# Second attention: the sum of squares of each head as one row, with a column of ones as weights

## What is computed

```python
    for blk in range(s // Q_BLOCK):
        ...
        weights = probs[:, :, 0] - lam * probs[:, :, 1]
        outs.append(jnp.einsum('bhqk,bkhe->bqhe', weights.astype(v.dtype), vb))
    o = jnp.concatenate(outs, axis=1)
    o = rms_norm(o, head_norm_g) * (1.0 - lam_0)      # mean of o*o over the 128 values of a head
    o = o.reshape(b, s, BRANCH) * jax.nn.silu(z)
    return x + o @ w_out
```

## Time and profile before

| what | value |
|---|---|
| median of 3 runs | 1300.03 us (1299.74 to 1300.12) |
| the profiled execution, its own time | 1300.48 us |
| its span in the trace | 1298.7 us |
| PE busy | 1289.9 us (99%), 7158 matmul records |
| PE weight loads busy | 1087.7 us (84%) |
| DVE busy | 793.3 us (61%) |
| ACT busy | 612.4 us (47%) |
| POOL busy | 299.9 us (23%) |
| DMA | 130.35 MB, mean 100 GB/s |

### The profile page before, as it was taken

The page is one execution under the profiler, slowest core; times in us unless marked ns, Lnnn a source line. Parts: engine busy times, 40 slices in busy tenths (PEclk is TensorE's granted clock), DMA queues, the critical chain, the costliest instruction groups (busy, mean ns, idle before and its releaser), DMA issues.

```text
span 1298.7 us, 18343 instructions
## 1 busy us (share of the span) xinstructions
PE 1289.9 (99%) x7158; PEld 1087.7 (84%) x7158; DVE 793.3 (61%) x1577; ACT 612.4 (47%) x1300; POOL 299.9 (23%) x203
## 2 busy tenths in 40 slices
PE   8999999999999999999999999999999999999999
PEld 6777888888889999999888887887888878887787
DVE  4435665333479887777333647576766667677743
ACT  4336654333435444445233445555556555656531
POOL 2022310000055656540001412122222213131110
PEclk9999999999999999999999999999999999999999
DMA  6322232332533334243236322222232222223511
GB/s 231 107 57 74 58 97 67 97 97 97 208 117 118 99 110 130 66 131 112 77 103 219 106 67 96 66 73 80 76 96 84 73 74 74 73 74 119 185 62 65
DMA packets 110297, 130.35 MB, mean 100 GB/s; under 512 B 7553, under 2 KB 87425, under 8 KB 110210
## 3 DMA queue, kind: packets, MB, share of 16 engines
q1 hardware_dynamic: 104450, 112.39, 26.9%
q10 hardware_dynamic: 5760, 16.78, 3.5%
HBM read 119.72 MB, written 9.44 MB: 99 GB/s over the span
## 4 chain that ended last, share of the span: by engine, by line
PE 93%; DVE 4%; issue 1%; ACT 1%; DMA 1%; POOL 0%; ACTq 0%; SPq 0%; DVEq 0%
PE ps L863 16%; PE ps L865 16%; PE ps L864 16%; PE ps L868 7%; PE ps L869 6%; PE ps L870 6%; PE ps L1087 4%; PE ps L1089 4%; PE ps L1090 4%; PE ps L1145 3%; DVE wlo L1524 2%; PE ps L1155 1%; PE ps L1127 1%; PE ps L1179 1%; PE ps L1169 1%
## 5 line engine op out<-in xcount | busy, mean ns | idle before, releaser
L1524 DVE TENSOR_TENSOR wlo<-raw,whi 128x512 fp32r<-128x512 f32 (+1 forms) x294 | 234.0, 822 | 178.5 <-ACT whi L1209 177.6
L1209 ACT ACTIVATE whi<-raw 128x512 fp32r<-128x512 f32 (+2 forms) x338 | 208.7, 650 | 118.0 <-PE ps L865 90.2
L863 PE MATMUL ps<-whi,hth 128*128 128x512 f32 x592 | 244.3, 413 | 0.0
L865 PE MATMUL ps<-wlo,hth 128*128 128x512 f32 x592 | 231.8, 392 | 0.0
L864 PE MATMUL ps<-whi,htl 128*128 128x512 f32 x592 | 231.2, 391 | 0.0
L1944 POOL TENSOR_TENSOR wlo<-raw,whi 128x384 fp32r<-128x384 f32 (+1 forms) x44 | 48.8, 1127 | 420.4 <-ACT whi L1209 420.4
L863 PEld LDWEIGHTS ps<-whi,hth 128*128 128x128 f32 x592 | 111.3, 188 | 31.0 <-issue 9.2
L865 PEld LDWEIGHTS ps<-wlo,hth 128*128 128x128 f32 x592 | 111.1, 188 | 25.0
L864 PEld LDWEIGHTS ps<-whi,htl 128*128 128x128 f32 x592 | 111.6, 189 | 19.0
L1474 ACT ACTIVATE px<-px,nm 128x128 f32<-128x128 f32 (+3 forms) x128 | 70.7, 554 | 90.2 <-DVE nm L1857 90.2
L868 PE MATMUL ps<-hth,whi 128*128 128x512 f32 (+1 forms) x288 | 111.9, 389 | 0.0
(11 more groups left out here) (347 smaller groups left out, 2861.3 us busy)
## 6 DMA issues: line engine op xcount, KB each, us to landing
raw<-in_l_w_in SPq DMA_DIRECT2D x64, 512.0 KB, 4.5
raw<-in_w_gate_up SPq DMA_DIRECT2D x44, 512.0 KB, 4.8
raw<-in_w_in SPq DMA_DIRECT2D x13, 1024.0 KB, 5.3
raw<-in_w_down SPq DMA_DIRECT2D x10, 1024.0 KB, 4.9
raw<-in_l_w_out SPq DMA_DIRECT2D x8, 1024.0 KB, 5.0
raw<-in_w_in SPq DMA_DIRECT2D x26, 256.0 KB, 3.3
raw<-in_w_branch SPq DMA_DIRECT2D x8, 512.0 KB, 3.9
raw<-in_w_out SPq DMA_DIRECT2D x4, 1024.0 KB, 4.8
```

Source lines behind the costliest of these rows:

```text
L863: e.matmul(o, ah, wh[:, cs], start=a, stop=False)
L865: m = e.matmul(o, ah, wl[:, cs], start=False, stop=z)
L1209: return e.activation(out, in_, ACT.Copy, **how)
L1524: return e.tensor_tensor(out, src, hi_part.bitcast(F32), ALU.subtract)
```

## The change

For heads 0 to 13 the sums are made the other way round: the squares move, and a column of ones (`ones_r`, 128x1, rounded to the fast format) is the weights. For this the squares are split in two: ScalarE copies the high part (`osh`) right behind the square, in `p2`; VectorE subtracts it (`osl`) in a new step `gl`. A new step `gr` makes two matmuls of 512 columns into one partition of a bank of its own. `gl` and `gr` stand ahead of `t2` part 0 of slot h+2. In `gr` ScalarE also copies the row from PSUM, times 1/128 and interleaved, into the first partition of `osq`, and starts a transfer of 2 KB that lays it over the 128 partitions as `hn` (128x4). GpSimd then waits for the transfer and adds the epsilon itself, in `gb`. VectorE's instruction of `gb` goes. Heads 14 and 15 keep the old way. The diff, cut:

```diff
@@ slot(h)
+        if out and now:
+            put("gl", h - 2)
+            put("gr", h - 2, self.bank())
         if last:
             put("t2", h - 1, 0, self.bank())
         yield
...
         if last:
             b = self.bank()
-            if out:
+            if h == H2:
                 put("ga", h - 2, b, 3 * P)
             put("t2", h - 1, 1, b)
-            if out:
+            if h == H2:
                 put("gb", h - 2, b, 3 * P)
+            elif out:
+                put("gb", h - 2, None, None)
@@ tensor
-                    free[b] = [(pt2_lo, 3 * h + i + 1)] + ([(hvar_d, h)] if i == 1 and h >= 1 else [])
+                    free[b] = [(pt2_lo, 3 * h + i + 1)] + ([(hvar_d, 1)] if i == 1 and h == H2 - 1 else [])
+                elif kind == "gr":
+                    h, b = a
+                    claim(b)
+                    pe.wait_ge(osh_a, h + 1)
+                    pe.wait_ge(osl_d, h + 1)
+                    pe.wait_ge(ones_rounded, 1)
+                    e.matmul(ps[b][0:1, :], ones_r[:, 0:1], osh[:], start=True, stop=False)
+                    e.matmul(ps[b][0:1, :], ones_r[:, 0:1], osl[:], start=False, stop=True).then_inc(ss_pe, 1)
+                    free[b] = [(row_a, h + 1)]
@@ scalar, "p2"
                     copy(oc[:], ps[b][:, :]).then_inc(oc_a, 1)
+                    act.wait_ge(osl_d, min(h, H2 - 2))
+                    act.wait_ge(hn_in, 16 * min(h, H2 - 2))
                     e.activation(osq[:], ps[b][:, :], ACT.Square).then_inc(oc_a, 1)
+                    if h < H2 - 2:
+                        act.wait_ge(oc_a, 2 * h + 2)
+                        act.wait_ge(ss_pe, h)
+                        copy(osh[:], osq[:]).then_inc(osh_a, 1)
+                elif kind == "gr":
+                    h, b = a
+                    act.wait_ge(ss_pe, h + 1)
+                    copy(row.rearrange("a (p q) -> a q p", q=TB), ps[b][0:1, :].rearrange("a (q p) -> a q p", p=P),
+                         scale=1.0 / P).then_inc(row_a, 1)
+                    act.wait_ge(row_a, h + 1)
+                    act.wait_ge(hpow_p, h)
+                    e.dma_start(hn[:, 0:4], row.rearrange("a (p q) -> a p q", q=TB)).then_inc(hn_in, 16)
@@ vector
+                elif kind == "gl":
+                    h, = a
+                    dve.wait_ge(osh_a, h + 1)
+                    dve.wait_ge(ss_pe, h)
+                    lower(osl[:], osq[:], osh[:]).then_inc(osl_d, 1)
+                elif kind == "gb" and a[0] >= H2 - 2:
...
@@ gpsimd, "gb"
                     pool.wait_ge(to_pe, h)
+                    if h < H2 - 2:
+                        pool.wait_ge(hn_in, 16 * h + 16)
+                        e.tensor_scalar(hn[:, 0:4], hn[:, 0:4], EPS, None, ALU.add).then_inc(hvar_p, 1)
+                        pool.wait_ge(hvar_p, h + 1)
+                    else:
+                        pool.wait_ge(hvar_d, h - H2 + 3)
                     e.tensor_tensor(hn[:, 4:8], hn[:, 0:4], neghalf[:, 0:4], ALU.pow).then_inc(hpow_p, 1)
```

More of the change, by code:

```diff
@@ L611, in build @@
         gh = sbuf(ctx, "gh", [P, 4])
-        st = sbuf(ctx, "st", [P, 64])
+        st = sbuf(ctx, "st", [P, 56])
         neghalf = sbuf(ctx, "neghalf", [P, 8])
         ones = sbuf(ctx, "ones", [P, 1])
+        ones_r = sbuf(ctx, "ones_r", [P, 1], F32R)
         raw = [sbuf(ctx, f"raw{i}", [P, 2048]) for i in range(3)]
@@ L681, in build @@
         osq = sbuf(att, "osq", [P, S])
+        osh, osl = (sbuf(att, n, [P, S], F32R) for n in ("osh", "osl"))
         v2h = [both(att, f"v2h{i}", [P, TB, 256]) for i in range(2)]
@@ L693, in build @@
         hn = sbuf(att, "hn", [P, 8])
+        row = osq[0:1, :]
         att.close()
@@ L772, in build @@
             sem(n) for n in ("ss_pe", "hvar_d", "hpow_p", "og_p", "to_pe", "ot_d2", "ot_hi", "ot_lo", "yo_d"))
+        ones_rounded, osh_a, osl_d, row_a, hn_in, hvar_p = (
+            sem(n) for n in ("ones_rounded", "osh_a", "osl_d", "row_a", "hn_in", "hvar_p"))
         SMALL = 16 * 14
@@ L1216, in _ @@
             act.wait_ge(const, 1)
-            e.activation(st[:, 62:63], neghalf[:, 0:1], ACT.Exp).then_inc(warm_a, 1)
+            e.activation(st[:, 54:55], neghalf[:, 0:1], ACT.Exp).then_inc(warm_a, 1)
             for s in STEPS:
@@ L1264, in _ @@
                     copy(id8[:], ident[:, 0:H1]).then_inc(id8_made, 1)
+                    act.wait_ge(ones_made, 1)
+                    copy(ones_r[:], ones[:]).then_inc(ones_rounded, 1)
                 elif kind == "qko":
@@ L1879, in _ @@
                     lower(ptl2[:, cs], ps[b][:, 0:n], pth2[:, cs]).then_inc(pt2_lo, 1)
-                elif kind == "gb":
+                elif kind == "gl":
[4 more added lines that the diff above has]
+                elif kind == "gb" and a[0] >= H2 - 2:
                     h, b, c = a
@@ L1883, in _ @@
                     dve.wait_ge(to_pe, h)
+                    dve.wait_ge(hpow_p, h)
                     e.tensor_scalar(hn[:, 0:4], ps[b][:, c:c + 4], 1.0 / P, EPS, ALU.mult, ALU.add).then_inc(hvar_d, 1)
@@ L2000, in _ @@
                     rb = hn[:, 4:8].rearrange("p (a d) -> p a d", d=1).to_broadcast([P, TB, P])
-                    pool.wait_ge(hvar_d, h + 1)
                     pool.wait_ge(to_pe, h)
+                    if h < H2 - 2:
[4 more added lines that the diff above has]
+                        pool.wait_ge(hvar_d, h - H2 + 3)
                     e.tensor_tensor(hn[:, 4:8], hn[:, 0:4], neghalf[:, 0:4], ALU.pow).then_inc(hpow_p, 1)
```

## The result

The changed kernel takes 1356.24 us (median; 1354.06 to 1356.42) against 1299.93 us before (1299.74 to 1300.12): ratio 1.0426, 95% interval 1.0414 to 1.0438. It is 56.3 us slower. The forecast was 39.0 us slower, 1339.0 us, in a range that ended at 1351. The sign and the place were right, the size was 17 us short.

The account below looks back on a forecast made before the run. TensorE, gapless in the second attention, was taken as the bound: 43.9 us of added waits less 4.9 saved made 39.0 us slower, 1339.0 us. Range 1333 to 1345 (67%), wider 1330 to 1351.

Parts of the forecast that it names:

- What bounds the kernel: Second attention: TensorE runs without a gap, so matmul time given up or waits added there count whole.
- The added waits: TensorE waits for VectorE's `osl` ahead of the new pair in slots 2 to 15, 43.9 us in all.
- the 0.55 us added for `osh`: Slot 14: ScalarE's copy `osh` stands ahead of work VectorE follows, adding 0.55 us to a wait of 4.9 us.
- two effects of unknown size: Slot 15: a further 0.4 us for `osh` and time won by slot 14's wait about cancel, leaving 1.6 us.
- The saving: New pair on TensorE takes 0.46 us against 0.81 for the old sums: 0.35 us a head, 4.9 us off.
- The drain: One-column pair might pay 0.09 us on each side, 2.5 us over 14 heads; the sum left it out.
- The clock falls (10%): Rival, 10%: after long waits TensorE comes back at 1.2 GHz; 1370 us, or 1353 at 2 us each.
- Backlog: Waits for `osl` repeat in each pair of slots; rival, 9%: odd waits lose 2 us each, giving 1327 us.
- What hides the rest: ScalarE's copies and issue, the transfer and POOL's addition fit into existing waits and room; cost nothing.
- The room of 3.9 us: Between the end of `og` at 1021.38 and TensorE's transposes of it at 1025.27 in the old trace.
- Faster (3%): Rival, 3%: VectorE reaches `osl` before TensorE asks, only the saving is left; 1295.1 us.

Follow-up runs that it names:

- experiment 4: Changed kernel with matmuls of unused result put on TensorE ahead of its wait for `osl`; 1339.7 us, ratio 1.0307 to the kernel before the change.
- experiment 6: The kernel of experiment 5 with the pair of new matmuls made twice for each of its 12 heads; 1305.21 us, ratio 1.0042.
- experiment 2: Changed kernel with `osl` left late in even slots 2 to 12 alone and moved a slot earlier elsewhere; 1328.26 us, ratio 1.0217.
- experiment 1: Changed kernel with only step `gl` moved, so that VectorE subtracts `osl` a slot earlier; 1305.41 us, ratio 1.0043 to the kernel before.
- the version with eleven heads: The code of experiment 5 with the new way for heads 0 to 10 only; 1296.75 us, ratio 0.9977 to the kernel before.
- experiment 3: Changed kernel with `osl` left late in odd slots 3 to 13 alone and moved a slot earlier elsewhere; 1338.84 us, ratio 1.0296.
- experiment 7: Changed kernel with the new way for heads 0 to 11 only, subtraction late where the change puts it; 1348.91 us, ratio 1.0377.
- experiment 5: Changed kernel with the new way for heads 0 to 11 only and the subtraction a slot earlier; 1301.21 us, ratio 1.0012.
- experiment 8: The kernel of experiment 5 with `osl` subtracted on POOL in place of VectorE; 1303.18 us, ratio 1.002 to the kernel before.
- experiment 9: The kernel of experiment 5 with ScalarE's copy `osh` made twice; 1302.12 us, ratio 1.0016 to the kernel before.
- experiment 10: Changed kernel with twelve heads the new way, `gl` late as in the change and `gr` later still, where `ga` stood; 1309.63 us, ratio 1.0071.

## Why the prediction was wrong, point by point

- **What bounds the kernel: right.** PE had no wait in this stretch, so each one added counted whole (experiment 4), and undoing the order took 51 us away, waits and clock together.
- **The added waits: right.** 43.9 us forecast, 42.7 measured. Even slots 1.95, measured 1.88 to 1.99; odd 4.28, measured 4.18 to 4.29; slot 14 4.9, measured 4.14: the 0.55 us added for `osh` did not come. Slot 15 1.6, measured 1.60, for which two effects of unknown size had been taken to cancel. The reading "start of the instruction that stood in that place before, less the moment PE asks" gave each within 0.1 us but for slot 14.
- **The saving: right.** The pair costs 0.47 us, 0.35 less than the sums. The drain that the Trainium skill (TensorEngine Tiling (Array Packing), Key Properties) gave reason to fear, taken as 0.09 us on each side, is not there: the steps into the pair and out of it are 0.23 us like the others (experiment 6).
- **The clock: the step that failed.** The text gave "The clock falls (10%)" and put the term at nothing in the sum, with "the stretches between waits are dense". In fact the granted clock halved at eight of the fourteen waits, for 17 us; with the clock kept up (experiment 4) the kernel takes 1339.7 us, the forecast's number. The mechanism, its place and its cause in the waits over 4 us were written down, and the price for "2 us each", 1353 us, was nearer than the forecast. What was wrong was the weighing: the wait of 2.8 us near the start, followed by transposes at half speed, was the only evidence on the question and pointed to the clock, though the granted clock is written as full there. And dense work after a wait did not keep the clock up: PE worked without a gap behind each of these waits. The sum's own uncertainty, 4.2 us either way and 2.5 us of the saving, gives 1334.8 to 1345.7 us, where the text has 1333 to 1345; neither this nor the wider 1330 to 1351 left room for the term.
- **Backlog: right for the changed kernel.** The waits repeat without shrinking. That they are independent was never claimed, but was assumed in the expectation of experiment 2, and there it was wrong by 6 of the 20 us; the rest was the clock and the tail.
- **What hides the rest: right in sum, wrong in size.** ACT's row copy took 1.08 us and not 0.6, the issue 0.48, and the transfer landed after 3.0 us (median) and not 2.0; POOL's addition took 0.23 us and not up to 1.03. The long waits covered it: PE waited 0.4 us once for the gate. The room of 3.9 us was read in slot 8 alone; in slot 14 the gate of the kernel before had 0.15 us. Once the waits were gone, the gate was the next bound, in slots 14 and 15.
- **"Faster (3%)", 1295.1 us with all 14 heads: not reached.** An early subtraction removes the waits the rival spoke of up to slot 13, but the tail's waits for the gate and for `osl` and the clock behind one of them take 10 us back (experiment 1).

## What to carry over

When a change makes TensorE wait, price the wait and then ask what the granted clock does after it: here waits of about 4.2 us cost 1.7 to 2.7 us more each. A new product can be placed by reading two times in the old trace, the moment the consumer asks and the moment the producer's queue gets there; move either end until they cross. Work that a stall hides is not free: cost the path through it (copy, issue, transfer, next engine) before removing the stall, and leave out the places where it has no room, as the version with eleven heads does.

## What the runs showed of the hardware

- After a wait of 4.14 to 4.36 us the granted clock fell every time, 19 times in the traces of the changed kernel and of experiments 3 and 7. After shorter waits it fell in some cases and not in others: in experiment 2 after 3.71, 3.63, 3.14 and 2.65 us, not after 2.63 and 2.82; in experiments 5, 6, 8 and 9 after gate waits of 3.0 us, not in experiment 10 after one of 2.6. A wait of 1.99 us (slot 2) was followed by a fall in the changed kernel and in experiment 7, and not in experiment 2; the waits of 1.88 us, five in the changed kernel and five in experiment 7, never were.
- Matmuls whose result nobody used, issued into the waits, kept the granted clock at 1.000 (experiment 4).
- A copy of 512 values on one partition, read or written with a stride, took ScalarE 1.08 us, against 0.60 for 128x512.
- A transfer of 2 KB from one partition to 128 landed 2.0 to 5.1 us after its issue in the changed kernel (median 3.0) and 3.6 to 5.4 us in experiment 5 (median 4.0).
- GpSimd's addition on 128x4 took 0.23 us (median) where its power on the same shape took 1.03.
